# Raw x columns, counted routing and whole down rows in a hybrid attention, SSD and expert kernel

## The reference, cut to what matters

```python
h = rmsnorm(x, g_mix);  proj = h @ w_in                 # x is 256 x 1024; q, k, v, pool, z, xs, B/C/dt, gates
x = x + (g0*(o_attn @ w0) + g1*(o_pool @ w1) + g2*(o_ssd @ w2)) @ w_mix_out
x = x + cross_attention(rmsnorm(x), rmsnorm(mem))       # 4 heads, 256 memory tokens
hf = rmsnorm(x)                                         # experts: top-1 of 4 groups, top-2 of its 4 experts
y = sum over 16 experts e of comb[:, e] * ((silu(hf @ w_gate[e]) * (hf @ w_up[e])) @ w_down[e])
return rmsnorm(x + y, g_final)                          # w_gate, w_up: 1024 x 512; w_down: 512 x 1024, all fp32
```

## Time and profile before

| what | value |
|---|---|
| median of 3 runs | 506.24 us (505.99 to 506.34) |
| profiled execution, first to last instruction (span) | 504.1 us |
| median less span: what lies around it, with the spread of the runs | 2.1 us |
| PE busy | 489.8 us, 97% |
| PE weight loads busy | 333.7 us, 66% |
| DVE, ACT, POOL busy | 249.4, 196.6, 15.7 us (49%, 39%, 3%) |
| moved by DMA | 149.28 MB, mean 296 GB/s |
| mean granted TensorE clock | 0.995 of full speed |

### The profile page before, as it was taken

How to read it: one execution, slowest core, us unless ns; L and a number is a source line. 1 busy time by engine, 2 the same in 40 slices (tenths; PEclk the granted TensorE clock), 3 DMA queues, 4 the chain that set the end, 5 groups by cost and what they waited for, 6 DMA issues and landing times.

```text
span 504.1 us, 7151 instructions
## 1 busy us (share of the span) xinstructions
PE 489.8 (97%) x2784; PEld 333.7 (66%) x2784; DVE 249.4 (49%) x469; ACT 196.6 (39%) x353; POOL 15.7 (3%) x30
## 2 busy tenths in 40 slices
PE   8999999999999999999999999999999999999993
PEld 8998998788888888878998534433443344433331
DVE  3764787988788689976664621111111111111113
ACT  5464667557626555345674211111211121111113
POOL 2000000000120000000100000000000000000000
PEclk9999999999999999999999999999999999999998
DMA  7797675543456448986799799999999999999992
GB/s 254 240 324 212 206 236 182 167 151 114 129 172 202 155 132 226 381 309 210 280 406 402 279 409 403 399 400 400 403 404 400 399 400 405 403 401 399 399 364 89
DMA packets 68026, 149.28 MB, mean 296 GB/s; under 512 B 8790, under 2 KB 15124, under 8 KB 67988
## 3 DMA queue, kind: packets, MB, share of 16 engines
q1 hardware_dynamic: 67684, 148.24, 81.0%
q10 hardware_dynamic: 304, 0.53, 0.3%
HBM read 147.69 MB, written 1.05 MB: 295 GB/s over the span
## 4 chain that ended last, share of the span: by engine, by line
PE 51%; issue 45%; DVE 2%; ACT 1%; POOL 0%; POOLq 0%; DVEq 0%; ACTq 0%
PE bank L1480 14%; PE bank L1481 14%; PE bank L1482 14%; PE bank L1487 2%; PE bank L1503 1%; PE bank L1591 1%; PE bank L1614 1%; PE bank L1587 1%; DVE al L957 1%; PE bank L1753 0%; PE bank L1736 0%; ACT ah L593 0%; PE bank L1776 0%; PE bank L1705 0%; PE bank L1745 0%
## 5 line engine op out<-in xcount | busy, mean ns | idle before, releaser
L971 DVE TENSOR_TENSOR wl<-raw,wh 128x1024 fp32r<-128x1024 f32 (+1 forms) x80 | 94.2, 1197 | 31.8 <-ACT wh L593 30.2
L593 ACT ACTIVATE wh<-raw 128x1024 fp32r<-128x1024 f32 (+1 forms) x80 | 81.5, 1041 | 55.7 <-PE bank L1482 40.3
L1480 PE MATMUL bank<-wh,ah 128*128 128x512 f32 (+2 forms) x248 | 95.1, 384 | 0.8 <-issue 0.8
L1481 PE MATMUL bank<-wl,ah 128*128 128x512 f32 (+2 forms) x248 | 93.3, 376 | 0.0
L1482 PE MATMUL bank<-wh,al 128*128 128x512 f32 (+2 forms) x248 | 93.3, 376 | 0.0
L1480 PEld LDWEIGHTS bank<-wh,ah 128*128 128x128 f32 x248 | 46.7, 188 | 9.3 <-issue 1.3
L1482 PEld LDWEIGHTS bank<-wh,al 128*128 128x128 f32 x248 | 46.6, 188 | 8.6
L1481 PEld LDWEIGHTS bank<-wl,ah 128*128 128x128 f32 x248 | 46.7, 188 | 7.8
L1480 PE MATMUL bank<-ah,wh 128*128 128x256 f32 x160 | 45.6, 285 | 0.6 <-DVE wl L971 0.4
L1481 PE MATMUL bank<-al,wh 128*128 128x256 f32 x160 | 45.3, 283 | 0.0
L1482 PE MATMUL bank<-ah,wl 128*128 128x256 f32 x160 | 45.3, 283 | 0.0
(11 more groups left out here) (372 smaller groups left out, 910.1 us busy)
## 6 DMA issues: line engine op xcount, KB each, us to landing
raw<-in_w_in SPq DMA_DIRECT2D x48, 512.0 KB, 5.0
wh_raw<-in_w_exp_up SPq DMA_DIRECT2D x13, 512.0 KB, 12.3
raw<-in_w_branch SPq DMA_DIRECT2D x12, 512.0 KB, 4.2
wl_raw<-in_w_exp_gate SPq DMA_DIRECT2D x12, 512.0 KB, 11.3
gates<-in_w_exp_gate SPq DMA_DIRECT2D x11, 512.0 KB, 11.1
raw<-in_w_exp_up SPq DMA_DIRECT2D x11, 512.0 KB, 12.5
gates<-in_w_exp_down SPq DMA_DIRECT2D x10, 512.0 KB, 10.6
gates<-in_w_exp_up SPq DMA_DIRECT2D x9, 512.0 KB, 11.1
```

The costliest lines, as they stand in the source:

```text
L593: act.activation(dst, src, ACT.Copy, scale=scale).then_inc(done, 1)
L971: dve.tensor_tensor(wl[:, n % RING, 0:sz], raw[:, n % RING, 0:sz], wh[:, n % RING, 0:sz].bitcast(F32), ALU.subtract)\
L1480: pe.matmul(dst, st[0], mv[0], start=start, stop=False, skip_group_check=True)
L1481: pe.matmul(dst, st[0], mv[1], start=False, stop=False, skip_group_check=True)
```

## The change

Eight edits. (1) x is transposed as it comes; the row scale of the first norm is applied where the projections leave PSUM, by two products that spread the scales over the partitions and by VectorE passes (`tokens_scaled`) for q, k, xs and pool. (2) The first two chunks are split in halves, and the warm-up begins with `ones`, with 13 products. (3) Routing counts for each logit how many of its group beat it. The softmax over groups moves behind the first gathers. (4) Two residual products move behind the ranks and behind the second gather; warm-up products at `x_o` and ahead of the ranks go. (5) Down weights of the first seven pairs come in units ("rows", pair, kt) of 128 whole rows (4 KB pieces), read in two steps, once for each half of the columns. (6) Products of neighbouring heads, and of the two B/C groups, alternate. (7) The combine weights of a pair take two products of full width. (8) The last squares and gains of the first column half move ahead of the last products; two stores instead of four.

The diff, cut to its core:

```diff
         if n < EXPERTS:
             out += [("gu", n, q) for q in range(4)]
-        if n >= lag:
+        if lag <= n and (n - lag) // 2 < PAIRS - 1 and n % 2 == 0:
+            out += [("rows", (n - lag) // 2, kt) for kt in range(4)]
+        if (n - lag) // 2 == PAIRS - 1:
             out += [("down", n - lag, j) for j in range(2)]
...
-WARM = (10, 6, 5, 6, 0, 0, 4, 4)
+WARM = (13, 0, 6, 6, 0, 0, 4, 4)
...
+        def used_up(u):
+            kind, n, j = UNITS[u]
+            if kind == "rows":
+                return rows_spent, ROWS_OF_PAIR * n + 1 + j + 1
+            return spent, SINGLE.index((kind, n, j)) + 1
...
+                if what == "rows":
+                    src = a["w_exp_down"][0, 2 * n + c % 2][P * j:P * j + P, :]
+                elif what == "down":
...
-                sp.dma_start(raw[:, n % RAW, 0:kn * cols].rearrange("p (k n) -> p k n", k=kn), src)\
-                    .then_inc(arrived[n % RAW], 16)
+                dst = raw[:, n % RAW, 0:kn * cols].rearrange("p (k n) -> p k n", k=kn)
+                if n == 0:
+                    sp.dma_start(dst[:, 0, :], src[:, 0, :]).then_inc(s_("head_in"), 16)
+                    sp.dma_start(dst[:, 1, :], src[:, 1, :]).then_inc(arrived[0], 16)
+                else:
+                    sp.dma_start(dst, src).then_inc(arrived[n % RAW], 16)
...
-                    sp.wait_ge(s_("cols_pe"), COLS["h"] + 4)
+                    sp.wait_ge(s_("sum_squares"), NORM["h"] + T)
...
-                    sp.wait_ge(spent, chunks[at - RAWX] // 2 + 1)
+                    sp.wait_ge(*used_up(chunks[at - RAWX] // 2))
...
+            sp.wait_ge(s_("final_rows"), 1)
+            sp.wait_ge(s_("final_rows_act"), 1)
+            sp.dma_start(out[0, 0:P, :], scaled[:, 0, :]).then_inc(stored, 16)
+            sp.wait_ge(stored, 16 * T)
...
+            act.wait_ge(s_("pool_step"), 1)
+            act.activation(table, ones[:, 0:1], ACT.Square)
+            act.wait_ge(s_("head_in"), 16)
+            head_hi(0, 0, s_("head_hi"))
             act.wait_ge(s_("g_cols_ready"), 1)
-            gained_cols_hi("h", g_cols)
-            for n in range(1, LEAD):
-                split(n)
+            gained_cols_hi("h", g_cols, (0,))
+            arrived_chunk(act, 0)
+            head_hi(0, 1, hi_done)
+            gained_cols_hi("h", g_cols, (1,))
+            arrived_chunk(act, 1)
+            head_hi(1, 0, s_("head_hi"))
+            head_hi(1, 1, hi_done)
+            gained_cols_hi("h", g_cols, (2,))
+            split(2)
+            gained_cols_hi("h", g_cols, (3,))
+            for t in range(T):
+                square_sum(x[:, t, :], h_ss[:, t:t + 1], hm[:, t, :], s_("sum_squares"))
...
-                if name == "q":
...
-                    copy_out("k", 1, kT[:, 2:4, :], 2)
...
-            act.wait_ge(s_("route_exp_arg"), 1)
...
-            act.activation(rt[4], rt[4], ACT.Exp).then_inc(s_("route_exp"), 1)
...
-                act.activation(combs[:, p % 2:p % 2 + 1], bank[2][:, 256:257], ACT.Copy).then_inc(s_("combs_ready"), 1)
+                for i, r in enumerate(row_half):
+                    ins = act.activation(combs[r, p % 2:p % 2 + 1], bank[2][r, 256 + i:257 + i], ACT.Copy)
+                ins.then_inc(s_("combs_ready"), 1)
...
+            cols_out(0, 2, bank[3], 3)
+            act.wait_ge(s_("route_exp_arg"), 1)
+            act.activation(rt[1][:, :, :], rt[1][:, :, :], ACT.Exp).then_inc(s_("route_exp"), 1)
...
             act.activation(table, ident[:, 0:1], ACT.Silu)
-            cols_out(0, 2, bank[3], 3)
...
+                if 2 <= n < EXPERTS:
+                    y_hi(p, bank[1], p + 1, rows_spent, ROWS_OF_PAIR * p + (ROWS_OF_PAIR if n % 2 else 1))
...
+                    for t in range(T):
+                        act.wait_ge(s_("scatter_pe"), T * (EXPERTS - 2) + t + 1)
+                        fin_squares_of(t, 0, fin_squares[:, t, :], s_("x_squares"))
...
-            for t in range(T):
-                mean_square(ss[:, t:t + 1], D, ss[:, t:t + 1], "h", t)
...
-                dve.tensor_scalar(hm[:, t, :], x[:, t, :], rs[:, t:t + 1], None, ALU.mult).then_inc(s_("h_rows"), 1)
...
+            def tokens_scaled(name, half, dst, done, scale=1.0):
+                j = bank_of(name, half)
+                dve.scalar_tensor_tensor(out=dst, in0=bank[j][:, :].rearrange("p (k n) -> p k n", k=2), scalar=scale, in1=h_rs_pair,
+                                         op0=ALU.mult, op1=ALU.mult).then_inc(done or free[j], 1)
+                return j
...
+            head_lo(0, 0)
+            gained_cols_lo("h", g_cols, (0,))
+            head_lo(0, 1)
+            gained_cols_lo("h", g_cols, (1,))
+            head_lo(1, 0)
+            head_lo(1, 1)
+            gained_cols_lo("h", g_cols, (2,))
+            split(2)
+            gained_cols_lo("h", g_cols, (3,))
+            for t in range(T):
+                mean_square(h_ss[:, t:t + 1], D, h_ss[:, t:t + 1], "h", t)
...
+                if name == "q":
+                    dve.wait_ge(s_("h_rs_pe"), 1)
+                    link(dve.tensor_copy(h_rs_row, pS1[:, 0:S]))
+                if name in ("q", "k"):
+                    dst, scale = (qT, 0.125) if name == "q" else (kT, 1.0)
+                    for half in range(2):
+                        tokens_scaled(name, half, dst[:, 2 * half:2 * half + 2, :], None, scale)
...
-            dve.tensor_reduce(top, lg[:, :, 0:4], AX.X, ALU.max)
-            link(dve.tensor_reduce(best1, expert_lg, AX.X, ALU.max))
...
-            link(dve.tensor_tensor(picked, first, second, ALU.add))
-            dve.tensor_tensor(by_group(chosen), by_group(picked), per_group(goh), ALU.mult).then_inc(s_("experts_chosen"), 1)
...
+            dve.tensor_tensor(level, rival, own, ALU.is_equal)
+            link(dve.tensor_tensor(beaten[:, :, :, 0:PER], rival, own, ALU.is_gt))
+            link(dve.tensor_tensor(beaten[:, :, :, PER:2 * PER], level, earlier, ALU.mult))
+            link(dve.tensor_reduce(rank[:, :, :].rearrange("p t (s e) -> p (t s) e", e=PER), beaten, AX.X, ALU.add))
+            link(dve.tensor_scalar(goh, rank[:, :, 0:4], 0.0, None, ALU.is_equal))
+            dve.scalar_tensor_tensor(out=by_group(chosen), in0=expert_rank, scalar=2.0, in1=per_group(goh), op0=ALU.is_lt, op1=ALU.mult)\
...
+            def softmax_arguments():
+                dve.tensor_reduce(top, lg[:, :, 0:4], AX.X, ALU.max)
...
+                dve.tensor_tensor(gap, best2, best1, ALU.subtract).then_inc(s_("route_exp_arg"), 1)
...
+            dve.wait_ge(s_("ranks_pe"), 2)
+            dve.tensor_copy(totals, bank[0][:, 0:EXPERTS]).then_inc(s_("totals_ready"), 1)
             for t in range(T):
                 moe_rows(t, D // 2, D)
             cols_out(0, 1, bank[2], 2)
+            softmax_arguments()
+            cols_out(0, 3, bank[2], 4)
             combine_weights()
-            cols_out(0, 3, bank[2], 4)
...
+            fin_gained_half(0)
             x_mean_square("fin")
-            gained(1, 1)
+            fin_gained_half(1)
             dve.wait_ge(s_("x_rstd"), X_NORM["fin"] // 4 + 1)
...
-                dve.tensor_scalar(scaled[:, 0, c], hm[:, 0, c], rs[:, 0:1], None, ALU.mult).then_inc(s_("final_rows"), 1)
...
-            keep_warm(WARM[0], bank[0])
...
+            pe.wait_ge(s_("pool_step"), 1)
+            for _ in range(WARM[0]):
+                pe.matmul(bank[0][:, 0:P], ones[:, :], ones[:, :], start=True, stop=True)
...
-            keep_warm(WARM[1], bank[1])
             for t in range(T):
-                pe.wait_ge(s_("h_rows"), t + 1)
+                pe.wait_ge(s_(f"x_in{t}"), 16)
                 for kt in range(KD):
                     mm = pe.transpose(rest[kt // 2][:, 256 * (kt % 2) + P * t:256 * (kt % 2) + P * t + P],
-                                      hm[:, t, P * kt:P * kt + P], ident[:, :])
+                                      x[:, t, P * kt:P * kt + P], ident[:, :])
...
+                if n < 2:
+                    for kk in range(kn):
+                        kt = 2 * n + kk
+                        pe.wait_ge(lo_done if kk else s_("head_lo"), n + 1)
+                        pe.wait_ge(s_("gained_lo"), GAINED["h"] + kt + 1)
+                        for j in range(4):
+                            mm = three(banks[j // 2][:, 256 * (j % 2):256 * (j % 2) + 256], [u[:, kk, P * j:P * j + P] for u in w],
+                                       [u[:, kt, :] for u in at], j % 2 == 0 and kt == 0, False)
...
+                if n == LAST["q"]:
+                    pe.wait_ge(s_("gained_lo"), GAINED["h"] + KD)
+                    pe.wait_ge(s_("rstd"), NORM["h"] + T)
+                    for t in range(T):
+                        mm = pe.matmul(pS1[:, P * t:P * t + P], h_rs[:, t:t + 1].to_broadcast([P, P]), ident[:, :], start=True, stop=True)
+                    mm.then_inc(s_("h_rs_pe"), 1)
...
-                    for g, dst in enumerate((pT, pO)):
...
+                    for at, (u, w_) in enumerate(((0, 0), (0, 1), (1, 1))):
```

(89 more changed lines are left out.)

227 lines of the change are left out of this document (101 added, 126 removed).

## The result

The changed kernel takes 514.0 us (median of 4 runs, 512.79 to 517.25) against 506.29 for the kernel before in the same session: a ratio of 1.0162, 95% interval 1.0129 to 1.0195, so 1.6% slower. The forecast was 511.4, its range 505 to 515.

The account below looks back on a forecast made before the run. It took TensorE and the weight transfers to end together in the expert stage. Later experts 5.8, sel_T 0.1, tail minus 0.7: 504.1 + 5.2 = 509.3, plus 2.1 for the median, 511.4; range 505 to 515.

Parts of the forecast that it names:

- SP's wait at ring place 11: Expert-stage refill: SP waits for the slot of pair 0's first row unit, some 16 us, about 307 to 323.
- the dry queue: Expert stage: queued transfers are done at 315.3 and data flow again from 324.7, so the engines stand dry 9.4 us.
- The hole: Expert-stage transfers: row units freed only in the next odd step stop the refill, leaving the DMA engines dry 9.4 us.
- the order: End of expert stage: 4 units instead of 6 follow the last gate/up unit, wanting it 5 us sooner in the stream.
- 481.4 for the last gate/up unit: Expert 15: 61 units at 2.564 us from 324.7, plus 0.3 to land; TensorE took this unit at 475.57 before.
- The front: Everything ahead of the experts: gains of 1.3 + 0.5 + 1.0 + 0.9 = 3.7 us, so expert 0 starts at 280.5.
- Start: From the transposes of x to the end of q: gain 1.3 us, between 0.5 and 2; q ends near 22.3.
- B/C products: Six products over 64 rows, alternated over the two row halves, can overlap: gain 0.5 us, between 0 and 0.6.
- Cross attention: Four warm-up products ahead of cross_out go and heads are taken side by side: gain 1.0 us, between 0.8 and 1.3.
- Routing: Logits to expert 0: counted ranks save 1.7 us, a moved residual product costs 0.9; gain 0.9, between 0 and 1.7.
- Rival 4: TensorE, waiting at gate/up units near the end, falls to half clock: 5 us or more, 516; chance 0.04.
- The tail: End of the kernel: 0.1 us from the halves, last of two stores issued 0.6 earlier; gain 0.7, between 0.2 and 1.2.

Follow-up runs that it names:

- e2: The kernel before with whole down rows as its only edit (two semaphores merged to make room): 518.93 us, ratio 1.0236.
- e1: The changed kernel with its down units in half columns (2 KB pieces) again, the rest of the change kept: 504.9 us, ratio 0.9964.
- e6: e1 with the residual products moved up by one, one of 512 columns between the two row tiles' logits: 501.94 us, ratio 0.9907.
- e10: The changed kernel with nothing but e6's order of residual products added: 514.14 us, ratio 1.0141.
- e4: The changed kernel, whole rows and unit order kept, each refill going to the ring place that comes free next: 505.38 us, ratio 0.9984.
- e8: e4 with pair 6 in half columns again, as in e3: 502.73 us, ratio 0.9917.
- after: The changed kernel with all eight edits, as profiled and measured: median 514.0 us, ratio 1.0162 to the kernel before.
- e5: e1 with the eight warm-up products of routing put back: 503.61 us, ratio 0.9957.
- e7: e1 with four final stores of 256 KB in place of two of 512 KB: 504.31 us, ratio 0.9957.
- e3: The changed kernel with pair 6, the last pair read by whole rows, in half columns again: 511.5 us, ratio 1.0092.

## Why the prediction was right, by its own steps

**The deciding edit was read rightly.** SP's wait at ring place 11 (forecast some 16 us, 307 to 323; measured 19.4, 304.6 to 324.0; the forecast had moved the end of the wait by its own 3.7 us of gain and left the start where it was), the dry queue (forecast 9.4 us from 315.3; measured 10 from 315), the place of the waits (experts 13 and 15 and the last rows, with one of 0.6 us at expert 11; 9.5 us, forecast 8), the pace (409 forecast, 409 measured). e2 shows that whole rows alone do it, and e1 that the other edits together lose nothing. The rule of the Trainium skill ("DMA: Bandwidth & Descriptors", Specifications) by which 2 KB and 4 KB pieces would cost the same is not borne out: 401 GB/s in the mixed stage with half columns, 409 with rows.

**The two causes of the delay.** The prediction gave the hole and the order together 5.8 us beside a front that gains 3.7, so 9.5 as a price. With the clock up they cost 12.2 (e6 to e10). e4 and e8 part them: closing the hole brings 8.6 us (after to e4), the order 2.8 us of waits (e4 to e8). The prediction called the order "5 us sooner in the stream" and the second part of the price; with the hole closed the stock covers nearly half of it.

**The size that was off** is the term "481.4 for the last gate/up unit": it came at 484.43, 3.0 later. The row unit was freed at 324.0 and not 323.3, as expert 0 started 0.65 later than forecast. The ramp behind the restart (344 GB/s from 325 to 330) cost 0.4. The rest, some 2 us, is the landing: I had allowed 0.3 us from the last byte to the product, and no row showed that figure. From 325.4 to 482 the trace has 407 GB/s, the bytes of 61 units; the product starts some 2 us behind. That the DMA engines work on bytes of the next units at the same time would explain it, and was not tried.

**The front** was to bring 3.7 and brought 3.0 in after's profile, 4.9 in e4's. The shifts are those against the kernel before. Start: forecast 1.3, measured 2.0 at the first score products (90.72 against 92.70), and 3.1 in e4's; the end of q is at 21.73, forecast 22.3. B/C products: their group shrank from 1.26 to 0.94 us, but at 162 us the shift is again what it was ahead of them (1.95 against 1.97), so nothing of the 0.5 arrived. Cross attention: 0.8 (shift 2.66 at the logits against 1.82 at 252 us), forecast 1.0. Routing: forecast 0.9, measured 1.1 in e4 (7.42 from the logits' end to expert 0, against 8.54 before) and 0.4 in after, whose clock was at half for 3 us. A step failed there: the term took the whole path at full clock and gave no reason. It is not that the warm-up products had held the clock up, since it fell in e2's profile with them in place, and in two of e5's eight runs the time and mean clock say the same. Rival 4 had a fall of the clock, but in the wrong place, where TensorE waits for transfers; there it stayed at 1.00, with waits of 1.6 us.

**The combine weights** were to cost 0.1 a pair. sel_T takes 0.58 to 0.71 us against 0.62 to 0.70: nothing.

**The tail** was to gain 0.7. From the last gate/up unit to the end it is 28.8 us against 28.5 before. From the second `y_last_hi` to the first scaled row it is 3.88 against 4.05, about the 0.1 that the prediction gave to the halves; the two larger stores bring nothing, as e7 shows. The term "four stores to two" was wrong.

**The sum.** Last unit +3.0, what follows it +0.8 (28.8 for a forecast 27.9), and the median stands only 0.8 over the profiled span where I had added 2.1, so -1.3: 511.4 + 2.5 = 513.9. The last term is luck: the profiled run, at 514.9, was one of the two slower ones of four. By the spans alone the forecast was 3.9 us short (509.3 against 513.2), 3.0 of it in the last unit.

## What to carry to other kernels

A buffer that serves two steps is held for two steps; in a ring refilled in order, everything that is free behind it waits too. Work out when each place is freed, and refill in that order: here that was worth more than 8 us with the same bytes in the same order. Ask of a hole in the transfers not whether anyone waits at that moment, but how much stock the consumer still has at the end.

## What was not expected of the hardware

TensorE's granted clock fell to 0.50 (1.2 GHz, from 2.4) with no idle time ahead of it. It fell at 271.8 (e1 and e3), 272.1 (e8), 273.2 (after) and 274.4 (e2), in the logits or just behind them; ahead of it the engine had been busy without a gap, with the products of cross_out, then with transposes and products of 20 columns. It did not fall in the profiles of e4, e5 and e7, which have the same logits. It stayed at half for 3 to 10 us, through the residual products and the ranks. The Trainium skill ("TensorE: Matmul & The Clock Gate", Part 1) ties the fall to the engine's idleness; by the profile's busy share, 1.00 in these stretches, the trace doesn't agree. What the chip itself counts as activity no run here shows. With e6's order, a product of 512 columns among the logits, the four profiles have 1.00 throughout and the 16 runs a mean of 0.992 and more; that it is this product and not the changed order behind the logits was not tried by itself. An idle stretch of 0.67 us behind the logits in e4 did no harm.
